# A two-layer float32 model on one core: the pooled stage turned round, and the modulation sums as columns

## The reference, cut to what matters

```
for gi, w in enumerate((2, 4, 8, 16)):                  # 256 features each
    cnt = minimum(t + 1, w)
    pooled = (csg - lag) / cnt - hf[..., lo:hi]           # csg: running sum over tokens; lag: the same w tokens ago
    outs.append(pooled @ pool_w[gi])                      # 256 x 256
return concatenate(outs, axis=-1) * pool_scale
...
h = rms_norm(x, norm_w) * (1.0 + scale) + shift
x = x + gate * y
```

## Time and profile before

| | |
|---|---|
| time, median of 3 runs | 957.27 us (956.63 to 958.1) |
| the profiled execution: time | 958.09 us |
| the profiled execution: span | 956.4 us |
| TensorE busy | 888.4 us, 93% |
| VectorE busy | 692.1 us, 72% |
| ScalarE busy | 456.8 us, 48% |
| HBM traffic over the span | 205 GB/s |
| TensorE, share of the chain that ended last | 81% |

### The profile page before, as it was taken

How to read it: one execution, slowest core, us unless ns; L and a number is a source line. 1 busy time by engine, 2 the same in 40 slices (tenths; PEclk the granted TensorE clock), 3 DMA queues, 4 the chain that set the end, 5 groups by cost and what they waited for, 6 DMA issues and landing times.

```text
span 956.4 us, 17671 instructions
## 1 busy us (share of the span) xinstructions
PE 888.4 (93%) x7028; PEld 852.6 (89%) x7028; DVE 692.1 (72%) x877; ACT 456.8 (48%) x573; POOL 58.0 (6%) x104
## 2 busy tenths in 40 slices
PE   2599999899999996799999999999999999999996
PEld 1388879799999996699999999988989999999996
DVE  4889878788878888766666556855487877776665
ACT  2347464566643333456663433444465444444445
POOL 2110110211111110000000000000000000000000
PEclk9789999999999996799999999999999999999998
DMA  9895755499989994057765555653435555654531
GB/s 336 300 339 193 244 200 177 130 319 322 317 306 330 330 316 134 23 184 234 239 199 176 175 183 168 197 166 130 157 90 177 177 179 187 218 173 158 169 126 44
DMA packets 156600, 196.60 MB, mean 206 GB/s; under 512 B 5341, under 2 KB 143116, under 8 KB 156556
## 3 DMA queue, kind: packets, MB, share of 16 engines
q1 hardware_dynamic: 142732, 145.64, 47.6%
q0 software_dynamic: 13824, 50.34, 14.4%
HBM read 194.90 MB, written 1.06 MB: 205 GB/s over the span
## 4 chain that ended last, share of the span: by engine, by line
PE 81%; DVE 9%; ACT 4%; issue 2%; DMA 2%; SPq 1%; DVEq 0%; ACTq 0%
PE G L557 15%; PE G L558 15%; PE G L559 15%; PE A L557 7%; PE A L559 7%; PE A L558 7%; DVE w_lo L1123 2%; ACT w_hi L1786 2%; PE G L632 2%; PE A L685 2%; PE G L633 2%; PE G L634 2%; DMA sinks<-in_attn_sinks_dram 1%; DMA MIX<-bias_rows 1%; DVE HN L1285 1%
## 5 line engine op out<-in xcount | busy, mean ns | idle before, releaser
L1123 DVE TENSOR_TENSOR w_lo<-raw,w_hi 128x2048 fp32r<-128x2048 f32 x135 | 307.1, 2275 | 163.7 <-ACT w_hi L1786 163.5
L1786 ACT ACTIVATE w_hi<-raw 128x2048 fp32r<-128x2048 f32 x135 | 256.6, 1901 | 265.7 <-PE A L559 132.4
L557 PE MATMUL G<-h_hi,w_hi 128*128 128x256 f32 x880 | 257.9, 293 | 22.5 <-DVE h_lo L1268 13.0
L558 PE MATMUL G<-h_lo,w_hi 128*128 128x256 f32 x880 | 253.3, 288 | 0.0
L559 PE MATMUL G<-h_hi,w_lo 128*128 128x256 f32 x880 | 253.2, 288 | 0.0
L557 PEld LDWEIGHTS G<-h_hi,w_hi 128*128 128x128 f32 x880 | 173.0, 197 | 29.5 <-issue 22.5
L558 PEld LDWEIGHTS G<-h_lo,w_hi 128*128 128x128 f32 x880 | 173.6, 197 | 0.2 <-issue 0.2
L559 PEld LDWEIGHTS G<-h_hi,w_lo 128*128 128x128 f32 x880 | 173.2, 197 | 0.0
L557 PE MATMUL A<-u_hi,w_hi 128*128 128x256 f32 x512 | 143.4, 280 | 0.7 <-DVE w_lo L1123 0.7
L558 PE MATMUL A<-u_lo,w_hi 128*128 128x256 f32 x512 | 142.9, 279 | 0.0
L559 PE MATMUL A<-u_hi,w_lo 128*128 128x256 f32 x512 | 142.9, 279 | 0.0
(11 more groups left out here) (325 smaller groups left out, 1315.7 us busy)
## 6 DMA issues: line engine op xcount, KB each, us to landing
raw<-in_mlp_w_dram SPq DMA_DIRECT2D x64, 1024.0 KB, 5.5
ada_raw<-in_ada_w_dram POOLq DMA_DIRECT2D x88, 512.0 KB, 5.7
raw<-in_w_in_dram SPq DMA_DIRECT2D x14, 1024.0 KB, 5.0
raw<-in_w_up_dram SPq DMA_DIRECT2D x11, 1024.0 KB, 5.4
raw<-in_w_gate_dram SPq DMA_DIRECT2D x11, 1024.0 KB, 5.3
raw<-in_attn_w_in_dram SPq DMA_DIRECT2D x9, 1024.0 KB, 7.1
raw<-in_w_down_dram SPq DMA_DIRECT2D x8, 1024.0 KB, 5.2
raw<-in_attn_w_out_dram SPq DMA_DIRECT2D x4, 1024.0 KB, 5.4
```

Source lines behind the costliest of these rows:

```text
L557: pe.matmul(dst, wh, ah, start=start, stop=False)
L558: pe.matmul(dst, wh, al, start=False, stop=False)
L1123: dve.tensor_tensor(w_lo[n % 2][:, 0:k, :], raw[n % RAW][:, 0:k, :], w_hi[n % 2][:, 0:k, :].bitcast(F32), ALU.subtract).then_inc(lo_done, 1)
L1786: act.activation(w_hi[n % 2][:, 0:k, :], raw[n % RAW][:, 0:k, :], ACT.Copy).then_inc(hi_done, 1)
```

## The change

**Column sums.** `turn_sums` and `part` are gone. All thirds are summed by `add_sums` as products with a column of ones, several thirds in one bank, and one VectorE operation (`thirds`) takes them. `sums1` takes shift and scale of modulation 1, `sums2` the gate of modulation 1 with shift and scale of modulation 2 between up(0) and down(0), `sums3` shift and scale of modulation 3.

**Pooled stage.** The mean over tokens and the product over features commute, so the product comes first. During down(0), x times the gain of modulation 2, without the root, is split into `h_hi` and `h_lo` tile by tile. TensorE multiplies them with the pool weights with tokens on the partitions (`pool_group`). The token's root comes later as a scalar per partition, and the shift's part is a row (`sw`) formed from the shift and the raw weights by ScalarE, VectorE and a product with ones: `z = rstd * G + sw`. Then the sliding means minus the token are a product of z with a constant band matrix (`band`, `band2`), in float32, which turns features back to the partitions. VectorE builds the band ahead of down(0) from a table of distances. The last tile of down(0) is written out of the loop: in it, VectorE forms the shift products, and takes its last two accumulations ahead of the residual.

```diff
-        take_each(("scale1a", 3), ("scale1b", 0), ("shift1a", 1), ("shift1b", 3), ("ms1", 2), ("gate1", 3),
-                  ("scale2", 3), ("ms2", 2), ("shift2", 3), ("gate2", 0), ("scale3a", 3),
-                  ("scale3b", 2), ("shift3a", 0), ("shift3b", 1), ("ms3", 3), ("gate3a", 2), ("gate3b", 3),
+        take_each(("sums1", 3), ("ms1", 2), ("sums2", 3),
+                  ("ms2", 2), ("sw0", 0), ("sw1", 1), ("gate2", 3), ("sums3", 3), ("ms3", 2), ("gate3", 3),
                   ("ms4", 2), ("ms5", 3))
...
 
-            def turn_sums(m, name, blocks):
-
...
-                    dst = bank_empty(pe, f"{name}{m}{'ab'[half]}")
-                    pe.wait_ge(ada_used, blocks)
-                    for t in range(4):
-                        at = (4 * half + t) * P
-                        last = pe.transpose(dst[:, t * P:(t + 1) * P], sums_of(m, part)[:, part, at:at + P],
-                                            ident)
-                    bank_done(f"{name}{m}{'ab'[half]}", last)
...
+                        last = pe.matmul(dst[:, k:k + 1], sq_sum[:, m, k * P:k * P + P], ones[:, 0:1],
+                                         start=m == 0, stop=m == 1)
+                bank_done(name, last)
...
                 pe.wait_ge(ada_used, blocks)
-                for t in range(DT):
-                    last = pe.matmul(dst[:, t:t + 1], sums_of(m, part)[:, part, t * P:(t + 1) * P],
-                                     ones[:, 0:1], start=True, stop=True)
-                bank_done(f"{name}{m}", last)
...
+                for n, (m, part) in enumerate(thirds):
+                    for t in range(DT):
+                        last = pe.matmul(dst[:, DT * n + t:DT * n + t + 1],
+                                         sums_of(m, part)[:, part, t * P:(t + 1) * P],
+                                         ones[:, 0:1], start=True, stop=True)
+                bank_done(name, last)
...
-            scale_and_shift(1)
+            add_sums("sums1", ((1, SHIFT), (1, SCALE)), ADA_C)
...
             up(0)
-            add_sums(1, "gate", ADA_D - 2)
+            add_sums("sums2", ((1, GATE), (2, SHIFT), (2, SCALE)), ADA_D)
             down(0)
-            add_sums(2, "scale", ADA_D)
-            mean_square(2)
-            add_sums(2, "shift", ADA_D)
-            add_sums(2, "gate", ADA_E)
...
             block_ready(N_POOL)
+
+            def pool_group(g):
+                pe.wait_ge(e2_ready, 2 * g + 2)
+                for k in range(2):
+                    u = U_POOL + 2 * (g // 2) + k
+                    if g % 2 == 0:
+                        g_empty(u)
+                    dst = halves(G[u % 4])[:, g % 2, :]
+                    toks = slice(k * P, k * P + P)
+                    for t in (2 * g, 2 * g + 1):
+                        pe.matmul(dst, h_hi[:, t, toks], w_hi[N_POOL % 2][:, t, :], start=t == 2 * g, stop=False)
+                        pe.matmul(dst, h_hi[:, t, toks], w_lo[N_POOL % 2][:, t, :], start=False, stop=False)
+                        last = pe.matmul(dst, h_lo[:, t, toks], w_hi[N_POOL % 2][:, t, :], start=False,
+                                         stop=t % 2 == 1)
+                return last
+
+            pool_group(0)
+            pool_group(1).then_inc(pool_done, 1)
+            pool_group(2)
+            token_sums("ms2", 2)
+            pe.wait_ge(sw_ready, 1)
+            for p in range(2):
+                pe.wait_ge((down_free0, down_free1)[p], 5)
+                dst = bank_empty(pe, f"sw{p}")
+                bank_done(f"sw{p}", pe.matmul(halves(dst), ones[:, :], HN[p][:, :, :], start=True, stop=True))
+            add_sums("gate2", ((2, GATE),), ADA_E)
+            pool_group(3).then_inc(block_used, 1)
...
             for g in range(4):
-                g_empty(U_POOL + g)
...
                 for m in range(2):
...
-            scale_and_shift(3)
+                    dst = halves(G[u % 4])[:, m, :]
+                    cols = slice(g * COLS + m * P, g * COLS + m * P + P)
+                    pe.matmul(dst[:, 0:P + POOL_PAD], z_tok[:, 0, cols], band[:, g, :], start=True, stop=False,
+                              skip_group_check=True)
+                    last = pe.matmul(dst[:, P:S], z_tok[:, 1, cols], band2[g], start=False, stop=True,
+                                     skip_group_check=True)
+                last.then_inc(band_done, 1)
+            add_sums("sums3", ((3, SHIFT), (3, SCALE)), ADA_E)
...
-            turn_sums(3, "gate", 96)
+            add_sums("gate3", ((3, GATE),), 96)
...
-            def part(m, name):
...
+                at = 3 * DT * m + DT * first
+                src = bank_full(dve, name)
+                bank_read(name, dve.tensor_tensor(
+                    MOD[:, :, :].rearrange("p m n -> p (m n)")[:, at:at + DT * count], src[:, 0:DT * count],
+                    V[:, V_ADAB + at:V_ADAB + at + DT * count], ALU.add))
+                bank_was_read(dve, name)
...
@@ -1513,86 +1527,94 @@
                         dve.tensor_tensor(u_lo[:, at, :], relu[j % 2][:, :, :], u_hi[:, at, :].bitcast(F32),
                                           ALU.subtract).then_inc(u_ready, 1)
                 if layer == 0:
-                    part(1, "gate")
+                    thirds("sums2", 1, GATE, 3)
+                    chain(factor(2))
+
+                    v = C[:, C_DIST:C_DIST + P + POOL_PAD]
+                    for g in range(4):
+                        chain(dve.tensor_scalar(band[:, g, :], v, -float(P), 1.0 / (2 << g), ALU.is_ge, ALU.mult))
+                        chain(dve.scalar_tensor_tensor(out=band[:, g, :], in0=v, scalar=float((2 << g) - P),
+                                                       in1=band[:, g, :], op0=ALU.is_lt, op1=ALU.mult))
+                        dve.tensor_tensor(band2[g], band[:, g, 0:P], ident, ALU.subtract)
...
+                    chain(dve.tensor_tensor(band[:, :, 0:P], band[:, :, 0:P], spread(ident, 4), ALU.subtract))
...
+                        if j == 2 and last:
+                            dve.wait_ge(sw_part, 1)
+                            for g in range(4):
+                                part = HN[g // 2][:, g % 2, :]
+                                at = 2 * g + 1
+                                ins = dve.scalar_tensor_tensor(out=part, in0=raw[N_POOL % RAW][:, at, :],
+                                                               scalar=MOD[:, 2, at:at + 1], in1=part,
+                                                               op0=ALU.mult, op1=ALU.add)
+                            ins.then_inc(sw_ready, 1)
                         if j < 3:
                             split_lo(n + 2, i)
-                        for _ in range((2, 2, 0, 0)[j] if with_ada else 0):
+                        for _ in range((2, 2, 2 if last else 0, 0)[j] if with_ada else 0):
                             ada_pair(1, done, i)
                             done += 1
                     for m in range(2):
                         residual_tile(layer, n, 0, m, MOD[:, 1 + 2 * layer, 2 * DT:], i)
...
+                    gain, hi, lo = (gain5, e_hi, e_lo) if layer else (GAIN[:, 2, :], h_hi, h_lo)
+                    for m in range(2):
+                        dve.wait_ge(e5_hi if layer else e2_hi, i * 2 + (m + 1))
...
+                        dve.scalar_tensor_tensor(out=lo[:, at, :].rearrange("p a s -> p (a s)"),
+                                                 in0=X[:, at, :].rearrange("p a s -> p (a s)"),
+                                                 scalar=gain[:, at],
+                                                 in1=hi[:, at, :].rearrange("p a s -> p (a s)").bitcast(F32),
+                                                 op0=ALU.mult, op1=ALU.subtract
+                                                 ).then_inc(e5_ready if layer else e2_ready, 1)
...
+                    for _ in range(6 - done if with_ada else 0):
+                        ada_pair(1, done, i)
+                        done += 1
+
+                with dve.Fori(0, 4 if layer else 3) as i:
+                    out_tiles(i, False)
+                if layer == 0:
+                    out_tiles(3, True)
...
-            for g in range(5):
-                if g < 4:
-                    tiles = slice(2 * g, 2 * g + 2)
-
-                    dve.wait_ge(pool_shifted, g + 1)
-                    src = H
-                    for n in range(g + 1):
-                        back = 1 << n
-                        into = (pad[1], win)[n % 2]
-                        chain(dve.tensor_tensor(into[:, tiles, POOL_PAD:], src[:, tiles, POOL_PAD:],
-                                                src[:, tiles, POOL_PAD - back:POOL_PAD + S - back], ALU.add))
-                        src = into
...
-            part(2, "gate")
+            for p in range(2):
+                if p == 0:
+                    dve.wait_ge(pool_done, 1)
+                else:
+                    dve.wait_ge(block_used, N_POOL + 1)
+                bank_was_read(dve, f"sw{p}")
```

(65 more changed lines are left out.)

152 lines of the change are left out of this document (54 added, 98 removed).

## The result

The changed kernel takes 975.47 us (median of 4 runs, 974.22 to 979.63) where the kernel before, beside it, takes 957.68: 1.0194 times as long, 95% interval 1.0159 to 1.0228. On a second occasion it took 972.87 (1.0173 [1.0147, 1.0199]). The profiled execution's span is 974.9 us against 956.4, 18.5 more. Slower was forecast, but by 12.05, not 18.5.

What follows compares the result with a forecast made beforehand. TensorE was taken to bound the kernel outside the small-operator stretches. The terms 0 + 0.5 + 1.8 + 1.5 + 16.6 + 0.3 - 12.6 + 3.0 + 0.95 gave +12.05 us, forecast 969.3 (chance 0.48), range 960 to 976.

Steps and rivals of the forecast that it cites:

- A: Opening sums (scale0, shift0): TensorE's added work offset by VectorE's saving; 0, bounds -0.6 and +0.5 us.
- B: gate0 in the attention: more TensorE work, less VectorE work; +0.5 us, bounds -0.3 and +0.9.
- C: sums1 before the first MLP: +1.8 us for 32 sums, +1.5 for a mean square at half clock.
- D: sums2 between up(0) and down(0): rest, 48 sums at half clock, slow start of down(0); +16.6 us, bounds +9.4 and +17.4.
- E: down(0) loop: added high and low parts on ScalarE and VectorE nearly fit; +0.3 us, bounds 0 and +2.
- F: Pooled stage, down(0) to up(1): -12.6 us from 39.8, +3.0 for the clock falling by the end of sums3.
- G: gate3 between up(1) and down(1): 8 transposes become 16 sums on TensorE; +0.95 us, bounds +0.8 and +1.
- 1: One-column products do not lower a full clock, so the clock terms 1.5 and 3.0 go; 964.8 us, chance 0.21.
- 2: Clock also falls inside the pooled stage, around the token sums, costing 5.0 us; 974.3 us, chance 0.16.
- 3: Not slower: clock holds over the 5.7 us rest and all one-column runs; 956.2 us, chance 0.06.
- 4: Pooled stage held up by the last tile's VectorE queue and slow, gain only 2; near 977 us, chance 0.05.

Runs made afterwards that it cites:

- 5: Kernel before, with only the gate sums at the first up/down boundary waiting for the last addition instead of the last but two; 968.38 us (1.010).
- 7: a_pad with sums2 divided in three (16 products behind up(0), 16 behind each of down(0)'s first two blocks) and earlier additions; 963.22 us (1.0037).
- 8: Kernel of 4 with sums2 divided in three, behind up(0) and the first two blocks of down(0), and earlier additions; 953.21 us (0.9939).
- 6: a_pad with the sums of modulations 1 and 3 taken against 32 columns of ones instead of 1; 968.98 us (1.0103).
- a_pad: Changed kernel with the dropped, unused 32-byte tile part_sums put back; 972.59 us (1.0172).
- 4: a_pad with the thirds of modulations 0, 1 and 3 transposed and reduced as before; 964.98 us (1.0063).
- 12: 8 with, in down(0)'s first three tiles, ScalarE's split before its high parts and VectorE's low parts after split and accumulations; 946.79 us (0.9878).
- 9: Kernel before with every tile behind part_sums 32 bytes lower, no instruction changed; 961.26 us (1.0038).
- 10: Kernel of 8 with the same 32 bytes taken away, no instruction changed; 954.96 us (0.9967).

## Why the prediction was right or wrong

The steps, forecast and in the profiled execution (us):

| step | forecast | measured |
|---|---|---|
| A, B: until sums1 begins | +0.5 | -0.1 |
| C: sums1 to up(0) | +3.3 | +5.05 |
| up(0) itself | 0 | +0.8 |
| D: end of up(0) to down(0) | +14.2 | +14.2 |
| D's slow start and E: down(0) | +2.7 | +5.8 |
| F: down(0) to up(1) | -9.6 | -10.2 |
| up(1) | 0 | -0.5 |
| G: gate3 | +0.95 | +0.97 |
| down(1) | 0 | +1.55 |
| the rest | 0 | +1.0 |
| sum | +12.05 | +18.5 |

**Part D, the largest term, held to a tenth**: rest 5.67, 48 products in 10.37, released by the addition on VectorE. That the rest alone costs its length and the clock is shown by 5, the whole by 7 and 8: with neither rest nor long run, 9.4 and 11.8 us come back. The band (292.29 to 297.9) lay hidden as told.

**Part F held**: 29.4 us, between the 27 and 31 named. The clock fell behind sums3, in the mean square, as told. The sums to up(1) cost 3.1 us over transposes, where +1.8 and +3.0 were told. gate3 ran from 511.79 for 1.92 us, as told.

**Part C was right in kind and too small.** Issue alone is +1.73 (6; told +1.8). The clock was told +1.5 with bounds to +1.9; it was +3.3, because it fell inside the run itself, so the sums slowed too (5.23 us for 3.63) besides the mean square. On the second occasion C was +2.7: the same program, another moment of the fall. The bound took in the mean square alone, though the same text had the fall as early as 2.1 us into a rest.

**Part E was the wrong step, and beside it stood a term put at nothing.** down(0) was told 2.7 us longer and is 5.8: 1.7 for the slow start (told 2.4), 2.5 for the spacing of the products (the next paragraph), and 1.6 for waits, where part E told 0.3. Part E followed one chain, split to split, found 0.1 us to spare and left the additions out. It did not follow the loop through the three slots: additions, refill, residual, bank. Beyond slow start and spacing TensorE loses 1.6 us over down(0) in the changed kernel, at 0.1200 us, but 3.8 in a_pad and in the kernel of 4, at 0.1168 and 0.1178. That is why a_pad's faster products won nothing in down(0): TensorE arrived sooner and waited longer. 12 confirms the loop by moving work only: beside its 3.4 us of sums it loses 0.3 where 8 loses 4.1.

**Not in the prediction at all: the place of the tiles.** The removed 32 bytes have no term in the sum. They slow the down products by 0.0033 us each: 768 x 0.0033 = 2.5 us in down(0), and less than that in down(1) and the last down stage (+1.55, +1.0), 5.1 in all and the largest part of the miss. 9 shows 3.2 us for the kernel before; in the changed kernel what it costs in down(0) would otherwise be waited by part E's loop, as a_pad shows.

**The tally.** The sum missed 6.5 us: 5.1 of place, 1.3 of waits in part E, 1.75 in part C and 0.8 in up(0), whose slow start lasts 6.0 us where it lasted 3.5 before. The slow start of down(0), part F, up(1) and parts A and B came out 2.4 below what was told. That the median still lies just inside the stated range (975.47 of 976) is luck: the range was made for the clock and two rivals, and neither place nor slots was among them.

**The rivals.** 1, one-column products do not lower the clock: refuted by 6, where only the number of columns differs. 2, the clock falls in the pooled stage: not in the changed kernel ahead of the mean square (no fall between 295.6 and 408.2), but in the kernels of 4, 6, 7 and 8, at 386.0, 386.3, 377.9 and 372.4. It came in the three first groups, earlier than told, and for less than the 5.0: they take 1.5 us longer. 3, not slower, wanted a boundary under 9 us; it was 14.2. 4, no gain in the pooled stage: it gained 10.2.

So the pooled stage turned round is a gain, which the sums as columns and their one place at the boundary turned into a loss; taken apart (8, 12) the change's idea beats the kernel before by 1.2%.

## What to carry to other kernels

Where a change adds small work to an engine's loop, follow the whole loop, through buffer slots and transfers back to the bank that the busiest engine waits for, not only the next handover. Work without a deadline goes behind the work that frees a slot. A sum that waits for the last of a stream is better divided and put among wide products than done in one run at a boundary where the busiest engine has nothing else.

## What the runs showed of the hardware

- For the clock, runs of one-column products were like rest, though TensorE shows 100% busy: it fell 1.9 and 4.4 us after sums1 and sums3 began (169.3, 408.2), and held with 32 columns at 0.111 us where one column had 0.109. Runs of 1.84 us of them between wide products did not lower it.
- The spacing of 256-column products depends on where the tiles lie: 0.1200 or 0.1167 to 0.1178 us, by 32 bytes per partition and no other difference (9 and 10). Between 0.1167 and 0.1178 something else decides, since a_pad has 0.1168 in down(0) and 0.1178 in down(1). What of the place matters was not tried; in the up stages it was 0.1200 in every kernel.
